# 88 tokens of the second half by gathered rows instead of 80 (sets of 64 and 24, 90 fetches of 128 rows for each table and layer), six row buffers, four blocks in the row tail, a third of v in full fp32

## The reference, cut to what matters

```
s  = einsum('thpd,pnd->thpn', q, sub_keys);   sv, si = top_k(s, 16)
cand = sv[:, :, 0, :, None] + sv[:, :, 1, None, :];   cv, ci = top_k(cand, 16)
experts = i1 * 128 + i2        # (256 tokens, 128 experts each)
gates = softmax(cv)
ub = take(u, eb);  a = gelu(einsum('td,tkd->tk', xb, ub)) * gb
vb = take(v, eb);  y = einsum('tk,tkd->td', a, vb)
x  = layer_norm(alpha * x + y)
```

## Time and profile before

| | |
|---|---|
| median of 3 executions | 1576.46 us (1574.13 to 1580.11) |
| the profiled execution, own time | 1579.14 us |
| its span, first to last instruction | 1577.3 us |
| TensorE busy | 1549.5 us, 98% |
| VectorE busy | 1355.4 us, 86% |
| ScalarE, GpSimd busy | 40%, 38% |
| moved by DMA | 493.95 MB, mean 313 GB/s |
| mean granted TensorE clock | 0.997 |

### The profile page before, as it was taken

How to read it: one execution, slowest core, us unless ns; L and a number is a source line. 1 busy time by engine, 2 the same in 40 slices (tenths; PEclk the granted TensorE clock), 3 DMA queues, 4 the chain that set the end, 5 groups by cost and what they waited for, 6 DMA issues and landing times. The chain is left out here.

```text
span 1577.3 us, 28052 instructions
## 1 busy us (share of the span) xinstructions
PE 1549.5 (98%) x10766; PEld 1494.5 (95%) x10766; DVE 1355.4 (86%) x2569; ACT 629.8 (40%) x1157; POOL 606.9 (38%) x438
## 2 busy tenths in 40 slices
PE   8999999999999999999999999999999999999998
PEld 8988999999999999999888899999999999999996
DVE  6987997989998998888956779898999888888895
ACT  4563222333334444544635341233333344444452
POOL 5651005644442555454003200265444435555520
PEclk9999999999999999999999999999999999999999
DMA  7644579999999999999833247799999999999990
GB/s 244 237 137 135 189 222 359 376 395 372 372 383 378 372 406 408 403 404 404 315 113 109 79 133 254 266 388 375 379 384 376 374 361 409 406 404 407 403 366 27
DMA packets 136965, 493.95 MB, mean 313 GB/s; under 512 B 16064, under 2 KB 16576, under 8 KB 136576
## 3 DMA queue, kind: packets, MB, share of 16 engines
q1 hardware_dynamic: 85248, 307.42, 52.3%
q0 software_dynamic: 47552, 170.06, 27.9%
q10 hardware_dynamic: 4032, 14.68, 2.6%
HBM read 488.79 MB, written 1.05 MB: 311 GB/s over the span
## 5 line engine op out<-in xcount | busy, mean ns | idle before, releaser
L690 POOL DMA_INDIRECT big<-v,picks x160 | 259.0, 1619 | 262.8 <-DVE big L1952 206.5
L690 POOL DMA_INDIRECT big<-u_rows,picks x160 | 220.4, 1377 | 245.9 <-DVE big L1868 217.3
L624 DVE TENSOR_TENSOR low<-raw,high 128x1024 fp32r<-128x1024 f32 x176 | 220.3, 1255 | 38.3 <-ACT high L1262 33.3
L728 PE MATMUL work<-columns,raw 128*128 128x176 f32 x1600 | 249.0, 313 | 3.2 <-DVE big L1846 3.2
L728 PEld LDWEIGHTS work<-columns,raw 128*128 128x128 f32 x1600 | 240.2, 190 | 3.7 <-issue 3.7
L1262 ACT ACTIVATE high<-raw 128x1024 fp32r<-128x1024 f32 x192 | 200.5, 1047 | 40.4 <-PE work L793 9.9
L1952 DVE SCALAR_TENSOR_TENSOR big<-big,side_hid 128x1024 f32<-128x1024 f32 x156 | 199.5, 1279 | 2.3
L1868 DVE SCALAR_TENSOR_TENSOR big<-big 128x1024 f32<-128x1024 f32 x160 | 190.4, 1218 | 9.3 <-DMA big<-u_rows,picks 9.3
L728 PE MATMUL work<-columns,extra_raw 128*128 128x176 f32 x1088 | 174.6, 317 | 5.0 <-DVE big L1846 4.3
L1530 ACT ACTIVATE xT<-big 128x176 fp32r<-128x176 f32 x198 | 67.5, 349 | 268.5 <-PE work L873 204.6
L728 PEld LDWEIGHTS work<-columns,extra_raw 128*128 128x128 f32 x1088 | 166.3, 193 | 5.5 <-issue 4.6
(11 more groups left out here) (262 smaller groups left out, 2881.8 us busy)
## 6 DMA issues: line engine op xcount, KB each, us to landing
raw<-u SPq DMA_DIRECT2D x150, 512.0 KB
raw<-v SPq DMA_DIRECT2D x146, 512.0 KB
extra_raw<-v SPq DMA_DIRECT2D x110, 512.0 KB
extra_raw<-u SPq DMA_DIRECT2D x106, 512.0 KB
raw<-wq SPq DMA_DIRECT2D x32, 512.0 KB
raw<-conv_in SPq DMA_DIRECT2D x14, 512.0 KB
aux<-ln_par ACTq DMA_DIRECT2D x9, 512.0 KB, 8.8
raw<-conv_out SPq DMA_DIRECT2D x8, 512.0 KB
```

The lines of the kernel that those rows point to most:

```text
L624: ops.tensor_tensor(low_at(c), raw_at(c), high_at(c).bitcast(F32), ALU.subtract).then_inc(low_made[RAW_SLOT[c]], 1)
L690: nc.gpsimd.indirect_dma_start(out=side_rows[n % SIDE_BUFS], out_offset=None, in_=rows, in_offset=bass.IndirectOffsetOnAxis(ap=pick_ids[:, ...
L728: mm = nc.tensor.matmul(out_, raw_at(c)[:, k * P:(k + 1) * P], x_full[:, k, :], start=(k == 0), stop=(k == KD - 1))
```

## The change

The side tokens become 88, in sets of 64 (2 groups, 64 fetches) and 24 (5 groups, 26 fetches): 90 fetches of 128 rows for u and 90 for v in each layer. The dense tokens become 168. In the second set 120 of the 128 partitions are used, but each fetch still moves 128 rows. A group's 26 picks can lie across the two halves of the table of picks, so one group's picks come in two copies (`pick_pieces`). Hidden values for 168 tokens leave room for six row buffers. The gates are spread in 21 batches. CHOSEN_AT goes from 26 to 27. The u pairs done in full are 28 instead of 27 (so 86 blocks of u are full instead of 84), the v blocks done in full are every third (39) instead of every fourth (29), and the row tail is 4 blocks, so that 124 v blocks go in columns.

```diff
-CHOSEN_AT = 26
-EXP_AT = 20
+CHOSEN_AT = 27
+EXP_AT = 21
...
-SETS = ((64, 2), (16, 8))
+SETS = ((64, 2), (24, 5))
...
-SET_ROWS = [PH * TOPK // _groups for _, _groups in SETS]
+SET_ROWS = [-(-PH * TOPK // _groups) for _, _groups in SETS]
+SET_USED = [_n * _groups for _n, _groups in SETS]
...
-BATCHES = DT // BATCH
+BATCHES = -(-DT // BATCH)
+GT = BATCH * BATCHES
...
-FULL_PAIRS = {5, 14, 23, 33, 42, *PAIR_OF}
+FULL_PAIRS = {7, 15, 21, 28, 35, 42, 47, *PAIR_OF}
...
+def pick_pieces(i, g):
+
+    lo, hi = SET_ROWS[i] * g, min(SET_ROWS[i] * (g + 1), PH * TOPK)
+    return [(a, b) for a, b in ((lo, min(hi, P // 2)), (max(lo, P // 2), hi)) if a < b]
...
-TAIL = 8
+TAIL = 4
...
-FULL_V = [_n for _n in range(FIRST_COLUMNS, COLUMNS - LAST_COLUMNS) if _n % 4 == 3]
+FULL_V = [_n for _n in range(FIRST_COLUMNS, COLUMNS - LAST_COLUMNS) if _n % 3 == 1]
...
-TURN_AFTER = (4, 2)
+TURN_AFTER = (4, 3)
...
+            nc.gpsimd.memset(picks[:], 0.0).then_inc(side_filled, 1)
+            nc.gpsimd.memset(side_hid[:], 0.0).then_inc(side_filled, 1)
...
             def combine_tail(first, norm, wait_block, wait_half=None):
 
+                count, slot = (TAIL, COLUMNS) if norm % 2 == 1 else (KD, 0)
+
                 def part(n, halves, sides=range(2)):
-                    return combine_block(n, first + n, n == 0, n == TAIL - 1, halves, sides)
-                for n in range(TAIL):
+                    return combine_block((slot + n) % KD, first + n, n == 0, n == count - 1, halves, sides)
+                for n in range(count):
...
-                V.scalar_tensor_tensor(rows, rows, 1.0, side_x[set_of(d)], ALU.mult, ALU.mult,
-                                       accum_out=side_hid[:, d:d + 1]).then_inc(side_used, 1)
+                used = SET_USED[set_of(d)]
+                V.scalar_tensor_tensor(rows, rows, 1.0, side_x[set_of(d)][0:used], ALU.mult, ALU.mult,
+                                       accum_out=side_hid[0:used, d:d + 1]).then_inc(side_used, 1)
```

More of the change, by code:

```diff
@@ L97 @@
 assert len(BATCH_OF) == BATCHES and len(SIDE_SUMS_AT) == SIDE_ROWS
+def pick_pieces(i, g):
+    lo, hi = SET_ROWS[i] * g, min(SET_ROWS[i] * (g + 1), PH * TOPK)
+    return [(a, b) for a, b in ((lo, min(hi, P // 2)), (max(lo, P // 2), hi)) if a < b]
+PICK_LOADS = [sum(len(pick_pieces(_i, _g)) for _g in range(SETS[_i][1])) for _i in range(len(SETS))]
 def set_of(d):
@@ L287, in gated_tokens @@
 def gated_tokens(pair):
-    return BATCH * sum(p <= pair for p in PAIR_OF)
+    return min(DT, BATCH * sum(p <= pair for p in PAIR_OF))
 def program(nc, x_rows, x_cols, positions, conv_par, diag, mla_par, ln_par, keys, w_uq, w_uk, w_uv,
@@ L667, in _ @@
                 pool.wait_ge(own_picked, layer + 1)
+                pool.wait_ge(side_filled, 2)
                 def fetch_picks(i, g):
[L670 to L674, removed]
+                    n, first_row = SETS[i][0], SET_ENDS[i] - SET_ROWS[i]
+                    for a, b in pick_pieces(i, g):
+                        half, to = divmod(a, P // 2)[0], first_row + a - SET_ROWS[i] * g
+                        at = a - half * (P // 2)
+                        nc.gpsimd.dma_start(
+                            picks[n * g:n * (g + 1), :, to:to + b - a],
+                            own_picks[SET_AT[i]:SET_AT[i] + n, :, half, at:at + b - a]).then_inc(picks_in[i], 16)
                 def fetch_tokens(i, g):
@@ L683, in _ @@
                     fetch_tokens(0, g)
-                pool.wait_ge(picks_in[0], 16 * SETS[0][1] * (layer + 1))
+                pool.wait_ge(picks_in[0], 16 * PICK_LOADS[0] * (layer + 1))
                 def gather(n):
@@ L898, in add_sides @@
             def add_sides(m):
-                for pick, total in zip(selector, side_sum):
-                    nc.tensor.matmul(y[:, 2 + m, :], pick, total[:, m * 512:(m + 1) * 512],
+                for pick, total, used in zip(selector, side_sum, SET_USED):
+                    nc.tensor.matmul(y[:, 2 + m, :], pick[0:used], total[0:used, m * 512:(m + 1) * 512],
                                      start=False, stop=False)
@@ L931, in combine_tail @@
                         pe.wait_ge(columns_sum, KD * (norm // 2) + 2)
-                    if norm % 2 == 1 and n == TAIL - 1:
+                    if norm % 2 == 1 and n == count - 1:
                         pe.wait_ge(columns_sum, KD * (norm // 2 + 1))
@@ L1936, in combine @@
                     step(V.memset(selector[i], 0.0))
-                    last = V.tensor_reduce(selector[i][:, SET_AT[i]:SET_AT[i] + n],
-                                           ident[:].rearrange("p (g t) -> p t g", t=n), AX.X, ALU.add)
+                    used = n * groups
+                    last = V.tensor_reduce(selector[i][0:used, SET_AT[i]:SET_AT[i] + n],
+                                           ident[0:used, 0:used].rearrange("p (g t) -> p t g", t=n), AX.X, ALU.add)
                 last.then_inc(selector_ok, 1)
                 def side_weighted(d):
-                    n, total = before + SIDE_ROWS + d, side_sum[set_of(d)]
-                    weight = side_hid[:, d:d + 1]
+                    used = SET_USED[set_of(d)]
+                    n, total = before + SIDE_ROWS + d, side_sum[set_of(d)][0:used]
+                    weight = side_hid[0:used, d:d + 1]
                     if d == 0:
```

25 lines of the change are left out of this document (14 added, 11 removed).

## The result

The changed kernel takes 1593.84 us (median of 4 executions, 1591.76 to 1598.09) against 1577.82 us for the kernel before on the same chip (4 executions): ratio 1.0103, 95% interval 1.0084 to 1.0122. It is slower by 1.0%, 16 us. I had forecast no change; the time lies in the range, at the place of the second rival (1594). The profiled execution of after is the fastest of its four, 1591.8 us with a span of 1590.0, so the two traces differ by 12.7 us and not by 16.

A forecast was written before the change was run, and what follows sets the result against it. TensorE and the transfers were within a few per cent, the transfers ending last and eating TensorE's gain. Per layer +0.9 - 2.7 = -1.8, twice -3.6, ends +1.4: -2.2 us, so 1575 us, range 1550 to 1598.

The forecast's parts named there:

- the second rival: Whole kernel: two full resources, TensorE and transfers, disturb each other; +8 us per layer, 1594 us, slower; chance 29%.
- TensorE's terms: Per layer, TensorE alone: u -11.4 us, v blocks 0 to 113 -7, behind block 113 -2.7; 21 us shorter.
- Its own path: TensorE's own stretch in u, choice to v: 262.5 - 11.4 = 251 us.
- the sum of the transfers from the choice to block 113: Choice to v block 113: 516.4 + 3.5 + 3 - 9 + 3 = 516.9 us, +0.9 per layer.
- The base: Choice to block 113: 210.7 MB take 519 us at 406 GB/s or 514 at 410; taken as 516.4 us.
- The credits: Choice to block 113: 4.5 us for blocks and rows landed ahead, 4.5 for the last fetches; 9 us saved.
- The losses: Choice to block 113: 3.5 us for copies of picks and tokens, 3 at v's start, 3 for late moments.
- late moments: Choice to block 113: slots full while TensorE or VectorE is late, 3 us, estimated from 3.8 us of waits.
- VectorE's 258 us of the forecast: In u: VectorE's 242 us of work plus 16 us of waits alone would hold the stretch at 258 us.
- the signs that I had named: Layer 1: 400 to 410 GB/s also in u; wrong if v reaches 415, or u stays under 390 while VectorE waits.
- The first rival: Whole kernel: transfers have more to give, 410 GB/s and above; 1543 to 1562 us, put at 1550; chance 27%.
- The sixth buffer: Start of v, where all buffers are full: cuts the loss there from 4.3 to 3 us.

The follow-up runs named there:

- both reliefs: Changed kernel with u's full blocks behind the choice loading half their columns and u's dots working on half their elements; 1559.73 us, ratio 0.9883.
- run 2: Changed kernel with the 57 full u blocks per layer behind the choice loading only half of their columns; 1595.28 us, ratio 1.0106.
- run 10: Changed kernel with five buffers for fetched rows instead of six; 1603.07 us, ratio 1.0153 to the kernel before.
- run 8: Changed kernel with the second set's fetches moving only the 120 used rows instead of 128; 1724.03 us, ratio 1.0923.
- the sets alone: Changed kernel with the 88-token sets but v as before, a quarter in full and eight blocks in rows; 1608.25 us, ratio 1.0172.
- v with fewer bytes (1): Changed kernel with the 39 full v blocks per layer loading only half of their columns; 1572.82 us, ratio 0.9960.
- shorter dots (3): Changed kernel with VectorE's 90 dots per layer working on 512 of 1024 elements, fetches unchanged; 1585.12 us, ratio 1.0044.
- more u pairs in full (9): Changed kernel with three more pairs of u blocks (30, 37, 44) multiplied whole; 1592.42 us, ratio 1.0091.
- a quarter in full (11): Changed kernel with one v block in four in full fp32 instead of one in three; 1600.04 us, ratio 1.0132.

## Why the prediction was wrong

**What held.** TensorE's terms: a full u block 2.28 us as worked out, narrow products no faster, a v block 2.18 us where nothing holds it (2.17 forecast), the tail 10.9 us shorter (11.0 forecast), and block 113 to the tail's end -2.6 and -2.8 us (-2.7 forecast). Its own path was right as well: with both reliefs choice to v takes 246 to 247 us, where I had 251. VectorE's work in u is 242 us, as forecast. The ceiling held: 406 GB/s in 200 us of v before and after. That the transfers end last held too, and they set v's pace.

**The step that failed** is the sum of the transfers from the choice to block 113, 516.9 us. It took 524.2 and 527.2 us, +7.0 and +11.6 instead of +0.9. The stretch of layer 0, then that of layer 1:

```profile
234.67:758.86 524.19, 501.38 (x3767) 492.94 (x3767) 465.40 (x630) 191.70 (x344) 272.12 (x196) 1.00 1.02 399
1011.30:1538.51 527.21, 503.88 (x3767) 494.81 (x3767) 459.76 (x611) 189.22 (x340) 272.64 (x196) 0.99 1.01 397
```

The bytes are near (about 209.2 MB in either; 210.7 forecast), the mean rate is not: 516.9 us need 408 GB/s, above the 406 that I had read over 200 us. Three terms make up the 7.3 and 10.3 us above 516.9:

- *The base.* I took the mean of 519 us (406 GB/s) and 514 us (410 GB/s, seen in 20 us only). The rate that lasted was 406, so 2.6 us were missing.
- *The credits,* 9 us for what was landed ahead and for the last fetches. The stretch moved 1.5 MB less than forecast, and that is 3.7 us: 5.3 us of credit did not come. What had landed ahead did help, but it was small. Blocks 4 to 20 of layer 1 ran at 2.18 us and blocks 20 to 113 at (1538.5 - 1319.8) / 93 = 2.35, so it was worth some 16 x 0.17 = 2.7 us.
- *The losses,* 3.5 us for the copies of picks, 3 for late moments, 3 at the start of v. Against 406 GB/s u lost (1 - 394 / 406) x 262.1 = 8 us in layer 0 and (1 - 391 / 406) x 264.4 = 10 in layer 1, v 1 and 2 us. Together 9 and 12 against 9.5. The 3 us for late moments, read from TensorE's 3.8 us of waits before, were too small in u: those waits grew to 13.9 us.

The largest mis-sized term is the credits. They stood against the losses and made the sum look like the time of before.

**In u** the picture that VectorE, TensorE and transfers lie side by side, with the slowest setting the time, held better than the raw times say. With the transfers relieved, as far as run 2 does it, VectorE holds the stretch at 264 to 267 us, with the dots halved the transfers hold it at 258 to 259, with both relieved TensorE holds it at 246 to 247. Less the time lost at the lower clock (table below) these are 259 to 260, 255, and 246 to 247, and the changed kernel has 260 to 261: the slowest of the three and about 1 us more. VectorE's 258 us of the forecast were nearly right. The forecast has no term for the clock; in the changed kernel it costs 1.7 and 3.4 us of u, in before 1.7 and 1.7. The longest wait for banks in layer 1 is VectorE's own backlog and not late rows: VectorE works without a break for over 8 us before this wait of 2.7 us ends (at 1186 us), and with the loads relieved the same wait is as long.

**The second rival** was right in kind for v. It was to decide once the mean rate from choice to block 113 stays under 400 GB/s: 399 and 397. Its v block was 2.34 us: 2.34 and 2.35. Its +12 less 4 for v came as +8.1 and +10.2, its -2.7 for the end as -2.6 and -2.8. Its +3 for u did not come (-1.1 and +1.4), so that its 1594 meets the median of 1593.84 is in part luck: of its +8 per layer the profile shows +4.4 and +8.8. Its 29% was too low. Of the signs that I had named, the rate in u stood between the two: 394 and 391 GB/s, under the forecast's 400 and above the 390 below which I would be wrong. The argument that I held against it, that 377 GB/s in u were what TensorE asked for, was true of before and said nothing of whether the 408 of the sum could be held over 517 us.

**The first rival** needed 410 GB/s or more in v with TensorE never idle. The rate stayed 406 with TensorE idle for 6.3 of 200 us, so it is refuted for this mix of loads and fetches. By the Trainium skill's "DMA: Bandwidth & Descriptors", section "Bandwidth" (425 GB/s), the stretch would have taken 496 us with TensorE as the bound; the trace disagrees, since no slice of after passes 409 GB/s.

**The sixth buffer** was given 1.3 us per layer at the start of v. The rate there did rise, from 326 to 378 GB/s, but with five buffers it is 366 (run 10), so the buffer gave about 22 x 12 / 406 = 0.7 us of it. Its worth, 3 to 4 us per layer, shows in u, which I had not looked at, and over half of that is clock.

**Left open:** why the clock falls behind a wait in one kernel and not behind the same wait in another (next section but one), and what 120 rows do to the packets (run 8).

## What to carry to other kernels

When a change takes work from an engine that is full and gives transfers to DMA engines that are also full, first divide the bytes by the best rate that the trace has held over a long stretch and ask what has to be true for less; a sum that ends above that rate is a forecast of something never seen. Credits that cancel the losses need a source as good as theirs. Where several bounds lie within a few per cent (here about 246, 255 and 260 us), relieving one only shows the next, so test each relief apart and all together. Before a stretch of one kernel is compared with that of another, take out what either lost at the lower clock.

## What was not expected of the hardware

**Fetches of 120 rows instead of 128** took the mixed rate of loads and fetches from 409 GB/s to between 271 and 279 with the DMA share unchanged (run 8).

**A wait of TensorE can cost more than its length.** In the kernel before, TensorE waits 2.15 us for banks in u of layer 1, and the 16 full products behind it take 4.13 us instead of 2.55. TensorE in order of time there:

```profile
1082.98 4.13 PE L728 MATMUL work<-columns,extra_raw 128*128 128x176 f32 x16 [2.15 <-DVE big L1846]
1086.94 2.55 PE L728 MATMUL work<-columns,raw 128*128 128x176 f32 x16
```

The same moment as a window (the granted clock is the number after the last parenthesis):

```profile
1084.00:1087.50 3.50, 3.50 (x18) 3.50 (x18) 1.81 (x5) 0.00 (x0) 2.57 (x3) 0.71 1.02 362
```

Behind this wait the clock record stands at the lower level (1.2 GHz) before it is back at 2.4, and that costs 1.6 us, nearly as much as the wait itself.

**The same wait costs this in one kernel and not in another.** At the same place of layer 1 the changed kernel and the sets alone both wait 1.99 us; the 32 products behind it, in the changed kernel and then in the sets alone:

```profile
1138.63 4.80 PE L745 MATMUL work<-columns,extra_raw 128*128 128x168 f32 x32 [1.99 <-DVE big L1867]
1153.17 6.48 PE L745 MATMUL work<-columns,extra_raw 128*128 128x168 f32 x32 [1.99 <-DVE big L1867]
```

The first 4 us behind the wait as windows, in the same order:

```profile
1138.60:1142.60 4.00, 3.97 (x28) 4.00 (x29) 4.00 (x8) 1.48 (x3) 3.10 (x3) 1.00 1.02 400
1153.20:1157.20 4.00, 4.00 (x17) 4.00 (x17) 4.00 (x8) 1.48 (x3) 3.09 (x3) 0.57 1.00 388
```

Both have ten waits of 1.5 us or more in the u stretches of the two layers. In the changed kernel the clock falls behind three of them, in the sets alone behind nine. From the clock records of the traces, layers 0 / 1, in us; "lost" is half of the time at the lower level (1.2 of 2.4 GHz), and taking it off is an estimate, as if TensorE had set the pace all that time:

| kernel | choice to first v block | lost to the clock | without it |
|---|---|---|---|
| before | 263.2 / 263.1 | 1.7 / 1.7 | 261.5 / 261.3 |
| changed kernel | 262.1 / 264.4 | 1.7 / 3.4 | 260.4 / 261.0 |
| v with fewer bytes (1) | 266.7 / 265.5 | 6.8 / 3.4 | 259.8 / 262.1 |
| u with fewer bytes (2) | 264.4 / 267.2 | 5.1 / 6.8 | 259.2 / 260.4 |
| shorter dots (3) | 258.2 / 259.0 | 3.4 / 3.4 | 254.8 / 255.5 |
| both reliefs (4) | 247.2 / 246.2 | 0 / 0 | 247.2 / 246.2 |
| sets of 88 alone (5) | 269.3 / 272.2 | 10.2 / 11.9 | 259.1 / 260.3 |
| more u pairs in full (9) | 264.9 / 262.9 | 5.1 / 3.4 | 259.8 / 259.5 |
| five buffers (10) | 266.3 / 267.3 | 5.1 / 5.1 | 261.2 / 262.2 |
| a quarter in full (11) | 266.7 / 266.8 | 5.1 / 5.1 | 261.6 / 261.7 |

The kernels with the code of the changed kernel in u (1, 5 and 11) differ there by up to 10 us, and by 3 once the clock is taken out. Of the 12.7 us that the changed kernel's profile is longer than before's, the clock in u is 1.7, and in the v columns the clock never falls in either; the slowdown itself is not the clock's.
